# GpSimd instead of TensorE adds each token's own row to the shared expert's rows

## What is computed

```python
def swiglu(x, w_gu, w_down):
    g, u = jnp.split(x @ w_gu, 2, axis=-1)
    return (jax.nn.silu(g) * u) @ w_down

# moe_ffn: top_idx, w from the router; per expert e: the tokens that chose it
    out = swiglu(x_pad[tok], w_exp_gu[e], w_exp_down[e]) * buf_w[:, None]
    routed = jnp.zeros((T + 1, D)).at[buf_tok].add(out)[:T]
    return routed + swiglu(x2d, w_sh_gu, w_sh_down)

# second_block
    ff = moe_ffn(x.reshape(B * S, D), ...)
    x = layer_norm_2(DEEPNORM_ALPHA * x + ff, ln3_g, ln3_b)
```

## Time and profile before

| | us |
|---|---|
| median of 3 runs | 2682.42 (2681.78 to 2683.23) |
| the profiled execution | 2681.46 |
| its span in the trace | 2679.5 |

### The profile page before, as it was taken

How to read it: one execution, slowest core, us unless ns; L and a number is a source line. 1 busy time by engine, 2 the same in 40 slices (tenths; PEclk the granted TensorE clock), 3 DMA queues, 4 the chain that set the end, 5 groups by cost and what they waited for, 6 DMA issues and landing times.

```text
span 2679.5 us, 34993 instructions
## 1 busy us (share of the span) xinstructions
PE 2603.9 (97%) x12355; PEld 2031.6 (76%) x12355; DVE 1963.6 (73%) x2844; ACT 1410.6 (53%) x2164; POOL 278.8 (10%) x242
## 2 busy tenths in 40 slices
PE   9999999999999999999999998999999999999996
PEld 7877878788887877888887775587667777777773
DVE  4788765777736985877736738456488999999996
ACT  4766652222324545322333233444456899898893
POOL 0000000000000000000000800000016622222210
PEclk9999999999999999999999999999999999999998
DMA  3222232222323123223233542323139999999997
GB/s 113 71 64 70 63 102 94 95 94 94 97 87 103 46 64 59 81 104 104 67 108 111 151 143 25 110 95 106 57 124 353 396 393 392 401 401 393 393 395 284
DMA packets 260215, 435.49 MB, mean 163 GB/s; under 512 B 45374, under 2 KB 199047, under 8 KB 235267
## 3 DMA queue, kind: packets, MB, share of 16 engines
q1 hardware_dynamic: 241795, 397.71, 42.0%
q0 software_dynamic: 18304, 36.26, 4.4%
HBM read 416.44 MB, written 42.62 MB: 171 GB/s over the span
## 4 chain that ended last, share of the span: by engine, by line
PE 85%; DVE 6%; DMA 3%; ACT 3%; issue 2%; DVEq 0%; SPq 0%; ACTq 0%; POOLq 0%
PE tp L1374 40%; PE tp L2081 4%; PE tp L2083 4%; PE tp L2082 4%; PE tp L1330 2%; PE tp L1480 2%; PE tp L1482 2%; PE tp L1481 2%; PE mp L2103 2%; PE mp L2105 2%; PE mp L2104 2%; PE tp L1421 2%; PE tp L2069 2%; PE tp L1879 1%; DMA uT<-in_w_exp_gu 1%
## 5 line engine op out<-in xcount | busy, mean ns | idle before, releaser
L1374 PE MATMUL tp<-sq_r,arena_r 128*128 128x512 f32 x1056 | 413.8, 392 | 5.8 <-DVE uT_r L2982 3.5
L1374 PE MATMUL tp<-uT_r,arena_r 128*128 128x512 f32 x1056 | 411.7, 390 | 0.0
L1374 PE MATMUL tp<-sq_r,wring_r 128*128 128x512 f32 x1056 | 411.7, 390 | 0.0
L1374 PEld LDWEIGHTS tp<-sq_r,arena_r 128*128 128x128 f32 x1056 | 198.6, 188 | 50.8 <-issue 7.3
L1374 PEld LDWEIGHTS tp<-sq_r,wring_r 128*128 128x128 f32 x1056 | 198.7, 188 | 41.7
L1374 PEld LDWEIGHTS tp<-uT_r,arena_r 128*128 128x128 f32 x1056 | 198.6, 188 | 41.3 <-issue 0.5
L2954 DVE TENSOR_TENSOR wring_r<-wring,arena_r 128x2048 fp32r<-128x2048 f32 x82 | 187.2, 2322 | 48.8 <-ACT arena_r L2244 48.5
L1374 PE MATMUL tp<-arena_r,wring_r 128*128 128x512 f32 x564 | 219.4, 389 | 0.0
L2492 ACT ACTIVATE arena<-arena 128x512 f32<-128x512 f32 x44 | 27.8, 633 | 288.1 <-DVE arena L3040 288.0
L2244 ACT ACTIVATE arena_r<-wring 128x2048 fp32r<-128x2048 f32 x82 | 152.2, 1902 | 39.4 <-DVE arena L3144 11.8
L3895 DVE TENSOR_TENSOR arena_r<-arena,arena_r 128x1024 fp32r<-128x1024 f32 x128 | 150.2, 1213 | 0.5 <-ACT arena_r L2839 0.5
(11 more groups left out here) (633 smaller groups left out, 6261.2 us busy)
## 6 DMA issues: line engine op xcount, KB each, us to landing
wring<-in_w_exp_gu SPq DMA_DIRECT2D x64, 1024.0 KB
arena<-in_w_exp_down SPq DMA_DIRECT2D x64, 1024.0 KB
uT<-in_w_exp_gu SPq DMA_DIRECT2D x32, 1024.0 KB
sq<-in_w_exp_gu SPq DMA_DIRECT2D x32, 1024.0 KB
wring<-in_f_up_w SPq DMA_DIRECT2D x22, 1024.0 KB, 5.0
wring<-in_f_up_w SPq DMA_DIRECT2D x44, 512.0 KB, 6.4
wring<-in_f_down_w SPq DMA_DIRECT2D x32, 448.0 KB, 5.3
wring<-in_a_in_proj SPq DMA_DIRECT2D x42, 256.0 KB, 2.7
```

The costliest lines, as they stand in the source:

```text
L1374: ins = nc.tensor.matmul(b[:], parts[wp][:, kk, m * P:(m + 1) * P], xparts[xp][:, kk, :], start=n_k == 0 and q == 0, stop=n_k == k - 1 and ...
```

## The change

1. TensorE's eight `own_row` products go. `shared_down(i, 0)` now starts the tile.
2. ScalarE evicts the tiles without scale (ALPHA is no longer applied here), and the tiles lie in another order: `raw` for tokens 0 to 255, `ye` for 256 to 511.
3. GpSimd has a new `own_row(i)`: it waits for the eviction of tile i and adds, in SBUF, the token's own row to it. The sum is written in place; the own row is read with a step of 128 elements (512 bytes). The tiles of tokens 256 to 511 lie on `row_tok[0]` and `row_tok[1]`, so ScalarE evicts tiles 4 and 5 only after additions 0 and 1, tiles 6 and 7 only after additions 2 and 3, and splits expert 0's down weights only after all eight.
4. SP writes a row block to `rest` after its two additions.
5. The index products 0 to 3 come after tiles 2 (first half), 0, 2 and 4 (second halves); the turn of expert 1's tokens comes in the middle of expert 0's products; VectorE's one-hot tiles and splits are placed to fit; GpSimd puts fewer table entries between the first gathers and more after gather 3.
6. ALPHA is applied at the end: VectorE's first addition becomes ALPHA x `fin` + rank 0 in one instruction.

```diff
-        rest_halves = [[y[:, 512 * half:512 * half + 512] for half in range(2)] for y in ye]
-        rest_halves += [[raw[2 * k + half][:, PAD:PAD + 512] for half in range(2)] for k in range(2)]
+        rest_halves = [[raw[2 * k + half][:, PAD:PAD + 512] for half in range(2)] for k in range(2)]
+        rest_halves += [[y[:, 512 * half:512 * half + 512] for half in range(2)] for y in ye]
...
             for c in range(TC):
-                sp.wait_ge(tile_evac, RES_TILES - 8 + 2 * c + 2)
+                sp.wait_ge(pool_tables, 4 + 1 + 2 * c + 2)
...
+            def own_row(i):
+                pool.wait_ge(tile_evac, RES_TILES - 8 + i + 1)
+                natural = rest_halves[i // 2][i % 2].rearrange("p (q k) -> p q k", k=NK)
+                by_feature = row_tok[i // 2].rearrange("p (k q) -> p q k", k=NK)
+                G.tensor_tensor(natural, natural, by_feature[:, 64 * (i % 2):64 * (i % 2) + 64, :], ALU.add).then_inc(pool_tables, 1)
+
             put_entries(range(0, 6))
             m_gather(0, 0, 0, 1)
-            put_entries(range(6, 8))
+            put_entries(range(6, 7))
             m_gather(1, 1, 1, 2)
-            put_entries(range(8, 9))
+            for i in range(4):
+                own_row(i)
             m_gather(2, 0, 2, 3)
+            for i in range(4, 8):
+                own_row(i)
             m_gather(3, 1, 3, 4)
-            put_entries(range(9, 14))
+            put_entries(range(7, 14))
...
-            for i in range(NBANK):
-                own_row(i)
             pe.wait_ge(rt["weights"], 4 + NK + 4)
             for i in range(NBANK):
-                shared_down(i, 0)
-                if i in (0, 3):
-                    m_idx(i // 3, i // 3, i // 3)
+                first_half(i)
+                if i == 2:
+                    m_idx(0, 0, 0)
...
-                if i in (1, 3):
-                    m_idx(2 + i // 2, 2 + i // 2, i // 2)
+                if i in (0, 2, 4):
+                    m_idx(1 + i // 2, 1 + i // 2, (1 + i // 2) % 2)
                 if i == 6:
                     m_turn(0, 0, 16)
             assert tiles.s == RES_TILES
-            m_turn(1, 1, 16)
-            m_gu(0, 0, 0)
+            m_gu(0, 0, 0, halfway=lambda: m_turn(1, 1, 16))
...
-            for c in range(TC):
-                for half in range(2):
-                    take(rest_halves[c][half], scale=ALPHA)
-                if c == 2:
-                    m_xhi(0, 0)
+            for i in range(7):
+                if i == 4:
+                    act.wait_ge(pool_tables, 4 + 1 + 2)
+                if i == 6:
+                    act.wait_ge(pool_tables, 4 + 1 + 4)
+                take(rest_halves[i // 2][i % 2])
+            m_xhi(0, 0)
+            take(rest_halves[3][1])
+            m_ghi(1, 1, 1, 32)
             m_xhi(1, 1)
-            m_ghi(1, 1, 1, 32)
             m_silu(0, 0)
+            act.wait_ge(pool_tables, 4 + 1 + 8)
             m_dhi(0, 0, 0, 16)
...
                 for c in range(TC):
-                    add_rows(c, rank_rows[0])
+                    chain.inc()
+                    V.scalar_tensor_tensor(fin[c], fin[c], ALPHA, rank_rows[0][:, c, :], ALU.mult, ALU.add).then_inc(dve_chain, 1)
+                    added[c] = chain.v
```

43 lines of the change are left out of this document (22 added, 21 removed).

## The result

The changed kernel takes 2686.74 us (median of 16 runs, 2684.26 to 2689.82), the kernel before 2682.36 us (2679.57 to 2684.12): the ratio is 1.0016, with an interval of 1.0009 to 1.0023. So it is some 4 us slower: a ratio of 1 lies outside the interval, though the loss is less than the 5.4 us that I had called telling from no change. The forecast was 2685.0, range 2678 to 2690. The time is inside and the mechanism is not the one forecast. The profiled execution took 2686.91 us, its span is 2685.2.

What follows compares the result with a forecast made beforehand. The loads were taken to bound the end, through the issue of expert 3's weights: GpSimd's last addition at 2031.8 plus 0.86 gives 2032.7, 2.7 us later, so 2681.5 + 2.7 = 2684.2, or 2685 on the median's scale; range 2678 to 2690.

Steps and rivals of the forecast that it cites:

- What bounds before: Over the experts: TensorE leads until the middle, then the loads fall behind and decide the end, by 2.1 us.
- the issue of expert 3's weights: SP's queue, behind the last shared rows: moves from 2029.94 to 2032.7, and the end moves with it, 2.7 us later.
- Removed: TensorE before the experts: eight identity products go, 13.8 us; TensorE is done near 2015 instead of 2028.
- None comes through: At expert 0's gating product: of the 13.8 us taken from TensorE, none arrives at this point.
- Price of an addition: GpSimd's 512-column addition read at a 512-byte stride: 1.80 us, from dense 1.27 plus ScalarE's surcharge of 0.53.
- Turns with VectorE: GpSimd's additions alternate with VectorE's splits: an addition meeting one waits about 1.1 us; last addition ends at 2031.8.
- The third case: GpSimd's additions: stride free and no turns taken with VectorE, weights issued at 2024.1, 2677 to 2680; chance 0.12.
- Gather 4: GpSimd's queue behind nine entries: issued near 2048.7, landing 7.9 us later, 1 to 2 us after TensorE wants it.
- the lead of 2.1: At the end of the experts: TensorE is 2.1 us ahead of the loads, covering most of gather 4's wait.
- TensorE sets the end: Rival over the whole kernel: TensorE, not the loads, bounds; its 13.8 us come through, 2668.6; chance 0.03.
- Expert 0's gating product: On TensorE, after VectorE's splits and remainders: starts near 2036.5, against 2035.75 before.
- The residual: VectorE's first four additions at the end also multiply: costs nothing, since VectorE then sits idle 5.97 us for a load.

Runs made afterwards that it cites:

- before_no_own: Kernel before without its eight identity products, so the tokens' own rows are left out and nothing replaces them: 2679.39 us, ratio 0.9992.
- spread: Changed kernel, GpSimd's queue only: four table entries ahead of gather 4, three between it and expert 0's scatter, then two a step: 2682.07 us, ratio 0.9992.
- between: Changed kernel, GpSimd's queue only: five table entries ahead of gather 4, then each step's gather, entries and only then scatter: 2682.01 us, ratio 0.9996.
- few_entries: Changed kernel with four table entries instead of nine between gather 3 and gather 4, the five others one per later step: 2684.15 us, ratio 1.0007.
- between_no_add: The kernel between with a bare signal in place of each GpSimd addition, own rows left out: 2680.48 us, ratio 0.9994 to the kernel before.
- between_linked: The kernel between with GpSimd waiting for its own addition behind each addition: 2687.77 us, ratio 1.0023 to the kernel before.
- linked: Changed kernel with GpSimd waiting for its own addition behind each addition: 2689.81 us, ratio 1.0030 to the kernel before.
- between_identity: The kernel between with the eight identity products back on TensorE and a bare signal for each GpSimd addition: 2688.40 us, ratio 1.0021 to the kernel before.

## Why the prediction was right in number and wrong in its reasons

- **What bounds before.** That TensorE and the loads are within 2.1 us of each other held: without the products TensorE comes 7.0 us earlier at expert 14, and in the same execution only 3.3 of them are left at the last turn (before_no_own). That the end follows the issue of expert 3's weights one to one fell: 3.4 us earlier in the changed kernel, 4 us slower; 7.9 us earlier in before_no_own, 2 to 3.5 us faster.
- **Removed.** The four products and the early first gather came as forecast: the additions start at 2011.07 (forecast 2010.8). "None comes through": that was said of expert 0's gating product, which came 1.85 us earlier. TensorE is ready for expert 4 2.0 us earlier (55.4 against 57.4). The rest goes into the three waits ahead of it and into the lower clock after two of them, for which the forecast had no term.
- **Price of an addition.** Forecast 1.80, measured 1.54 to 1.56. ScalarE's surcharge for the stride (0.53) was the wrong row to borrow from: GpSimd's is 0.27 to 0.36. The estimate from the cycles in the Trainium skill (GPSIMD Engine Reference, Performance pitfalls for Q7 kernels), weighed ahead of the run, was 0.43; the trace is below it and nearer to it than to my row.
- **Turns with VectorE.** This step failed. I let one split in between two additions, from the earlier trace rows, where GpSimd waits for a semaphore after each operation; here GpSimd was not slowed, and VectorE stood for 5.88 us and most of 8.54. The last addition ended at 2026.14, not 2031.8, and expert 3's weights went out 3.4 us earlier, not 2.7 later. So the forecast delay of this issue, the one term that the 2685 was made of, had the wrong sign.
- **The third case** (stride free, no turns) comes nearest to this issue (2024.1, measured 2026.54) and gives 2677 to 2680. The next step kept the kernel from it, but not alone: with almost no gather late, spread and between still take 2682.
- **Gather 4.** This is the term that was mis-sized: 1 to 2 us, covered by the lead of 2.1. Its issue (2048.7, measured 2049.15) was right by luck: the last addition ended 5.7 us earlier than forecast, and the nine entries took 0.6 us each more than 1.67, 5.4 in all. The landing took 9.83 us and not 7.9 (the median of the scatters, which go up to 10.0), TensorE was ready 1.55 us earlier than I let it be, so the stall was 5.97 us, and I had no term for the half clock after it, 12.52 - 9.80 = 2.7 us. Together 8.7 us; less the 2.0 us by which TensorE was earlier, that makes 6.7 (6.5 measured at expert 14, both counted from the first entry), and less the 2.3 of load stalls 4.4. The two errors, 6 us too much in the issue and 7 too little in the gather, left the time at 2686.7 against 2685.0. That the number came out is luck.
- **TensorE sets the end** was a case at 2668.6 with all 13.8 us coming through. TensorE does set the end, but later than before. I had no case in which TensorE ends up later.
- **Expert 0's gating product** came at 2033.90 (forecast near 2036.5, before 2035.75): VectorE got free at 2028.4 and not after 2031.8.
- **The residual** costs nothing: shown twice.

## What to carry to other kernels

Work moved off a busy engine changes the order and the pace of its new engine's queue: look at each thing that the new owner must deliver on time (here a gather per step), and price its lateness by the stall and the slow clock after it, not by the lead at the end. If two streams are within a few us of each other, a cut on one of them can bring little more than that (here 13.8 us of products, 2 to 3.5 us), so measure the cut with the work left out before building its replacement. Small bookkeeping operations (here table entries) belong where their queue would stand anyway, and moving five of them ahead of one gather cost 11 us.

## What the runs showed of the hardware

- GpSimd's additions without a semaphore wait between them hold off VectorE's two-input operations for the whole block: 5.88 us for an operation on 128x1 behind four additions, 4.52 us behind four dense ones, 1.41 us where GpSimd waits for its own semaphore after each. The Trainium skill (SBUF — State Buffer, sections "SBUF: two separate sides" and "Who interferes with whom") says that a VectorE instruction with two SBUF inputs contends with a GpSimd instruction that reads SBUF, and that the one that starts first gets the ports for its whole instruction. The trace agrees on who blocks whom and shows a hold four instructions long.
- The other way round, GpSimd's indirect transfers took from under 1 to 3.56 us to issue. From 1996 to 2140 us there are 42 of 3.47 to 3.56 us in eleven of the fourteen kernels. All begin 0.07 to 0.15 us after the start of a gating product on VectorE and end 0.83 to 0.90 us after the two splits behind it (L3907, two SBUF inputs, 2.35 us), whatever VectorE does then: they seem to stand for both splits and then do their own 0.9 us. Six others that began at the same point took 0.98 to 1.01 us, one of them in the kernel before (2035.88). What let these through is not shown.
- After the stall of 1.78 us in between, TensorE's next step took 11.30 us instead of 9.80, at a mean granted clock of 0.85, and so did (11.28 us) the step after 1.61 us in few_entries; after stalls of 1.74 us in few_entries and 1.97 us in spread the next step lost no more than its own wait and 0.3 us. After 2.02 us in between_no_add, after 4.28 and 4.46 us in between_linked and linked, and after 5.97 us and more in the others, the clock was at its lower level at once (1.73 to 1.76 us for the turn instead of 0.93), but not after 2.44 us in between_identity and 2.89 in between_linked (0.99 us, and 1.5 us lost in the step). So the length of the stall alone doesn't tell what it costs.
- A gather of 112 rows issued into the full stretch took 9.83 us to land with a scatter issued 2.2 us behind it.
